# Feed-forward columns computed feature-major instead of token-major in a three-layer fp32 block kernel

## The reference

```
def _rmsnorm(x, w):
    x32 = x.astype(jnp.float32)
    y = x32 * lax.rsqrt(jnp.mean(x32 * x32, axis=-1, keepdims=True) + RMS_EPS)
    return (y * w.astype(jnp.float32)).astype(x.dtype)
...
u = _rmsnorm(h, norm_ffn_w[l])
hid = jax.nn.silu(jnp.einsum('btd,df->btf', u, w_ffn_gate[l])) * jnp.einsum('btd,df->btf', u, w_ffn_up[l])
h = h + jnp.einsum('btf,fd->btd', hid, w_ffn_down[l])
```

## Time and profile before

| | before |
|---|---|
| median of 3 runs | 2542.1 us |
| profiled execution | 2540.26 us, span 2538.5 us |
| TensorE products busy | 2493.6 us (98%), 14496 |
| TensorE weight loads busy | 2140.1 us (84%) |
| VectorE busy | 1802.3 us (71%) |
| ScalarE busy | 1154.8 us (45%) |
| mean granted clock of TensorE | 0.996 |
| DMA | 605.72 MB, 239 GB/s |

### The profile page before, as it was taken

One profiled execution on the slowest core, in us unless ns is written; L12 is line 12 of the kernel. 1 busy time (PEld: TensorE's weight loads), 2 busy tenths in 40 slices (PEclk: granted clock), 3 DMA queues, 4 the chain that ended last, 5 costly groups with the idle time before them and its releaser, 6 DMA issues.

```text
span 2538.5 us, 38110 instructions
## 1 busy us (share of the span) xinstructions
PE 2493.6 (98%) x14496; PEld 2140.1 (84%) x14496; DVE 1802.3 (71%) x2341; ACT 1154.8 (45%) x1476; POOL 0.2 (0%) x4
## 2 busy tenths in 40 slices
PE   8999999999999999999999999999999999999998
PEld 8977888788888888888888888899988788999886
DVE  6897676776677877777777777777786665546666
ACT  5544333464544544444443334433486344335642
POOL 0000000000000000000000000000000000000000
PEclk9999999999999999999999999999999999999999
DMA  7777676786778888888887788888745556675464
GB/s 218 247 248 255 213 256 217 264 272 215 254 237 268 286 286 283 284 282 282 282 286 259 261 262 263 279 288 282 248 141 185 183 175 185 188 235 181 133 219 146
DMA packets 317516, 605.72 MB, mean 239 GB/s; under 512 B 27310, under 2 KB 31412, under 8 KB 315708
## 3 DMA queue, kind: packets, MB, share of 16 engines
q1 hardware_dynamic: 301628, 571.59, 69.6%
q10 hardware_dynamic: 15744, 32.15, 3.6%
HBM read 593.03 MB, written 10.62 MB: 238 GB/s over the span
## 4 chain that ended last, share of the span: by engine, by line
PE 90%; DVE 4%; ACT 2%; DMA 2%; issue 1%; ACTq 0%; SPq 0%; DVEq 0%
PE bank L681 22%; PE bank L683 22%; PE bank L682 22%; PE bank L706 5%; PE bank L708 5%; PE bank L707 5%; PE bank L624 2%; PE bank L811 1%; DVE w_lo L1960 1%; ACT w_hi L1308 1%; DVE conv_out L2108 1%; DMA gemv_w<-in_w_mod 1%; DVE gemv_acc L1979 1%; DMA gates<-spill 1%; PE bank L1144 1%
## 5 line engine op out<-in xcount | busy, mean ns | idle before, releaser
L1960 DVE TENSOR_TENSOR w_lo<-raw,w_hi 128x1024 fp32r<-128x1024 f32 x820 | 1001.8, 1224 | 658.9 <-ACT w_hi L1308 656.8
L1308 ACT CAST w_hi<-raw 128x1024 fp32r<-128x1024 f32 x820 | 860.2, 1051 | 1290.2 <-PE bank L683 953.2
L681 PE MATMUL bank<-w_hi,u_hi 128*128 128x512 f32 x1216 | 483.5, 398 | 0.1
L683 PE MATMUL bank<-w_hi,u_lo 128*128 128x512 f32 x1216 | 474.3, 390 | 0.0
L682 PE MATMUL bank<-w_lo,u_hi 128*128 128x512 f32 x1216 | 474.0, 390 | 0.0
L1979 DVE SCALAR_TENSOR_TENSOR gemv_acc<-gemv_w,small,gemv_acc 128x512 f32<-128x512 f32 x480 | 358.8, 747 | 30.6 <-DMA gemv_w<-in_w_mod 25.3
L681 PE MATMUL bank<-w_hi,s_hi 128*128 128x512 f32 x744 | 297.9, 400 | 1.8 <-DVE w_lo L1960 1.7
L683 PE MATMUL bank<-w_hi,s_lo 128*128 128x512 f32 x744 | 291.4, 392 | 0.0
L682 PE MATMUL bank<-w_lo,s_hi 128*128 128x512 f32 x744 | 290.7, 391 | 0.0
L706 PE MATMUL bank<-s_hi,w_hi 128*128 128x256 f32 x1024 | 287.8, 281 | 0.3 <-DVE w_lo L1960 0.3
L707 PE MATMUL bank<-s_lo,w_hi 128*128 128x256 f32 x1024 | 287.6, 281 | 0.0
(11 more groups left out here) (365 smaller groups left out, 2858.9 us busy)
## 6 DMA issues: line engine op xcount, KB each, us to landing
gemv_w<-in_w_mod SPq DMA_DIRECT2D x384, 256.0 KB, 3.3
raw<-in_w_in SPq DMA_DIRECT2D x176, 512.0 KB, 4.5
raw<-in_a_w_in SPq DMA_DIRECT2D x128, 512.0 KB, 4.6
raw<-in_w_ffn_gate SPq DMA_DIRECT2D x88, 512.0 KB, 4.6
raw<-in_w_ffn_up SPq DMA_DIRECT2D x88, 512.0 KB, 4.6
raw<-in_w_ffn_down SPq DMA_DIRECT2D x88, 512.0 KB, 4.3
gemv_w<-in_kv_w_mod SPq DMA_DIRECT2D x128, 256.0 KB, 3.7
raw<-in_kv_w SPq DMA_DIRECT2D x64, 512.0 KB, 3.7
```

Of the source, the lines that this page charges most:

```text
L681: pe.matmul(o, xh, w_hi[pr.ring][:, s, t], start=(k == 0), stop=False)
L683: ins = pe.matmul(o, xl, w_hi[pr.ring][:, s, t], start=False, stop=(k == 2 * units - 1))
L1308: act.copy(w_hi[ahead.ring][:, s], raw[:, s]).then_inc(hi_done, 1)
L1960: dve.tensor_tensor(w_lo[ring][:, s], raw[:, s], w_hi[ring][:, s].bitcast(F32), ALU.subtract).then_inc(lo_done, 1)
```

## The change

The product "ffn" goes the second way. A body still computes one chunk of gate columns and one of up columns from the same weights, but now with 24 products of 256 columns in a unit in place of 12 of 512, and the four blocks of 128 hidden features come out with features on partitions, as down needs them. The transposes of `stage`, their PSUM banks and the waits for them are gone.

The root is now needed along the free dimension, on all partitions. VectorE writes a diagonal matrix for each half of the tokens (`root_diag`, identity times root), TensorE multiplies it with a matrix of ones behind unit 6 of the first body, and VectorE copies the result to `root_rows`. Both chunks are multiplied with it as they leave PSUM (`times_root`); ScalarE takes Silu of the gate chunk in place in slot 9, VectorE multiplies both at the end of the body, ScalarE casts the result in slot 2 of the next body and VectorE takes the low part in slot 4. `root_rows` lies where the causal mask and the not yet used `modc` lie, so the mask is loaded again before v2. Several semaphores are shared under new names (`staged`, `split_high`, `split_low`, `small_sum`).

```diff
+        root_rows = place("root_rows", [P, T], F32, at[0] + 4 * CAUSAL)
         keep = place("keep", [P, KEEP_W], F32)
+        modc = place("modc", [P, P], F32)
         cols = place("cols", [P, 3 * P], F32)
-        modc = place("modc", [P, P], F32)
...
+        root_diag = stage_all[:, 2 * COLS:2 * COLS + T]
+        hidden = stage[:, 1].rearrange("p h c -> p (h c)").rearrange("p (f t) -> p f t", t=T)
...
-            ("ffn", FF // COLS, 16, 2), ("down", 2, KF, 0),
+            ("ffn", FF // COLS, 16, 0), ("down", 2, KF, 0),
-        PASSES_ACROSS = ("qkv", "k2", "q2", "k3", "q3")
+        PASSES_ACROSS = ("qkv", "ffn", "k2", "q2", "k3", "q3")
...
                     if j == 1 and first:
                         last_x("w_out", "ffn")
-                    elif j == 3 and not first:
-                        turn_stage(pr, i - 1, 1)
-                chunk(pr, i, 0, u2_hi, u2_lo, pr.units // 2, due, {6: pr.turn0} if first else None)
-                chunk(pr, i, 1, u2_hi, u2_lo, pr.units // 2, due)
+                    elif j == 6 and first:
+                        pe.wait_ge(signal("over_root"), HALVES)
+                        pe.matmul(bank[SPARE][:, 0:T], ones, root_diag, start=True, stop=True).then_inc(signal("small_sum"), 1)
+                across_chunk(pr, i, 0, u2_hi, u2_lo, due, {6: pr.turn0} if first else None)
+                across_chunk(pr, i, 1, u2_hi, u2_lo, due)
...
                 if j == 3:
-                    turn_stage(pr, pr.bodies - 1, 1)
                     first_mods()
+                if j == KF // 2 - 3:
+                    pe.wait_ge(signal("split_low"), H1 + pr.bodies)
...
-            def silu_gate(pr, i, x):
-                if x == 0:
-                    act.wait_ge(signal("over_root"), 1)
-                    for th in range(HALVES):
-                        act.activation(stage[:, 0, th], acc[0][th][:], ACT.Silu, scale=sm(RR + th)).then_inc(drained[0], 1)
+            def silu_gate(j, i):
+                if j == 9:
+                    act.wait_ge(drained[0], i * 2 + 2 * (pr.body0 + 1))
+                    act.activation(stage[:, 0], stage[:, 0], ACT.Silu).then_inc(signal("gates_open"), 1)
             def hidden_high(j, i):
-                if j == 4:
-                    his_of_stage(products["ffn"], i, 1, hid_hi)
+                if j == 2:
+                    act.wait_ge(signal("staged"), i + (HALVES * products["branch"].bodies + 1))
+                    act.copy(hid_hi[:, ds(i * 4, 4)], hidden).then_inc(signal("split_high"), 1)
...
+            act.dma_start(keep[:, CAUSAL:CAUSAL + P], keep_const[:, CAUSAL:CAUSAL + P]).then_inc(signal("dist_in"), 16)
             act.dma_start(dist[:], keep_const[:, DIST:DIST + T]).then_inc(signal("dist_in"), 16)
...
                 if j == HALVES + 2:
                     dve.wait_ge(signal("root_x"), 2)
-                    dve.reciprocal(sm(RR, HALVES), sm(RR, HALVES)).then_inc(signal("over_root"), 1)
-            def times_gate(pr, i, x):
+                    own.link(dve.reciprocal(sm(RR, HALVES), sm(RR, HALVES)))
+                    for th in range(HALVES):
+                        dve.tensor_scalar(root_diag[:, th * P:(th + 1) * P], ident, sm(RR + th), None, ALU.mult).then_inc(
+                            signal("over_root"), 1)
+                if j == HALVES + 5:
+                    dve.wait_ge(signal("small_sum"), 2)
+                    own.link(dve.tensor_copy(root_rows[:], bank[SPARE][:, 0:T]))
+            def times_root(pr, i, x):
+                for half in range(2):
+                    dve.tensor_tensor(two_blocks(stage[:, x, half]), two_blocks(acc[x][half][:]), over_heads(root_rows[:], 2),
+                                      ALU.mult).then_inc(drained[x], 1)
                 if x == 1:
-                    dve.wait_ge(signal("over_root"), 1)
-                    dve.wait_ge(drained[0], i * 2 + 2 * (pr.body0 + 1))
-                    for th in range(HALVES):
-                        dve.scalar_tensor_tensor(out=stage[:, 1, th], in0=acc[1][th][:], scalar=sm(RR + th),
-                                                 in1=stage[:, 0, th], op0=ALU.mult, op1=ALU.mult).then_inc(drained[1], 1)
+                    dve.wait_ge(drained[1], i * 2 + 2 * (pr.body0 + 1))
+                    dve.wait_ge(signal("gates_open"), i + (2 * products["branch"].bodies + 1))
+                    dve.tensor_tensor(stage[:, 1], stage[:, 1], stage[:, 0], ALU.mult).then_inc(signal("staged"), 1)
             def hidden_low(j, i):
                 if j == 4:
-                    los_of_stage(products["ffn"], i, 1, hid_lo, hid_hi)
+                    blocks_of = ds(i * 4, 4)
+                    dve.wait_ge(signal("split_high"), i + (H1 + 1))
+                    dve.tensor_tensor(hid_lo[:, blocks_of], hidden, hid_hi[:, blocks_of].bitcast(F32), ALU.subtract).then_inc(
+                        signal("split_low"), 1)
...
-            dve.wait_ge(signal("dist_in"), 16)
+            dve.wait_ge(signal("dist_in"), 32)
```

More of the change, by code:

```diff
@@ L854, in delta_net @@
                 pe.matmul(bank[SPARE][0:H1, 0:T], small[0:BUCKETS, RELB:RELB + H1], early[0:BUCKETS, ONEHOT:ONEHOT + T],
-                          start=True, stop=True).then_inc(signal("rel_sum"), 1)
+                          start=True, stop=True).then_inc(signal("small_sum"), 1)
                 yield from rest(10)
@@ L1129, in down_first @@
                 if j == 3:
-                    turn_stage(pr, pr.bodies - 1, 1)
                     first_mods()
+                if j == KF // 2 - 3:
+                    pe.wait_ge(signal("split_low"), H1 + pr.bodies)
                 if j == products["down"].units // 2 - 1:
                     mod_columns(0)
-            turning_x("down", hid_hi, hid_lo, "v2", down_first, {KF // 2 - 2: pr.turn0 + pr.bodies * pr.turns})
+            pe.wait_ge(signal("split_low"), H1 + pr.bodies - 1)
+            turning_x("down", hid_hi, hid_lo, "v2", down_first, None)
             def scores2(p, a):
@@ L1585, in yb_high @@
                 act.wait_ge(signal("b_out"), h + 1)
-                act.copy(yb_hi[:, h], bank[OUTS][:, 0:T]).then_inc(signal("yb_high"), 1)
+                act.copy(yb_hi[:, h], bank[OUTS][:, 0:T]).then_inc(signal("split_high"), 1)
             def rows_in(hg):
@@ L1723, in norm_due, with first_ffn, ffn_due @@
                     root(0, sm(SS, HALVES), sm(RR, HALVES), 1.0 / D, E6, "root_x")
[L1725 to L1736 removed]
+            def silu_gate(j, i):
+                if j == 9:
+                    act.wait_ge(drained[0], i * 2 + 2 * (pr.body0 + 1))
+                    act.activation(stage[:, 0], stage[:, 0], ACT.Silu).then_inc(signal("gates_open"), 1)
+            def hidden_high(j, i):
+                if j == 2:
+                    act.wait_ge(signal("staged"), i + (HALVES * products["branch"].bodies + 1))
+                    act.copy(hid_hi[:, ds(i * 4, 4)], hidden).then_inc(signal("split_high"), 1)
+            def first_ffn(j):
+                norm_due(j)
+                silu_gate(j, 0)
+            def ffn_due(j, i):
+                hidden_high(j, i - 1)
+                silu_gate(j, i)
+            body("ffn", 0, nothing, first_ffn)
             with act.Fori(1, pr.bodies - 1) as i:
[L1738 removed]
+                body("ffn", i, nothing, lambda j: ffn_due(j, i))
             last = pr.bodies - 1
[L1740 removed]
+            body("ffn", last, nothing, lambda j: ffn_due(j, last))
             def mod_rows_in(n):
@@ L2480, in hidden_low @@
             def hidden_low(j, i):
                 if j == 4:
-                    los_of_stage(products["ffn"], i, 1, hid_lo, hid_hi)
-            body("ffn", 0, times_gate, norm_due)
+                    blocks_of = ds(i * 4, 4)
+                    dve.wait_ge(signal("split_high"), i + (H1 + 1))
+                    dve.tensor_tensor(hid_lo[:, blocks_of], hidden, hid_hi[:, blocks_of].bitcast(F32), ALU.subtract).then_inc(
+                        signal("split_low"), 1)
+            body("ffn", 0, times_root, norm_due)
@@ L2485, in _ @@
             with dve.Fori(1, pr.bodies - 1) as i:
-                body("ffn", i, times_gate, lambda j: hidden_low(j, i - 1))
+                body("ffn", i, times_root, lambda j: hidden_low(j, i - 1))
             last = pr.bodies - 1
-            body("ffn", last, times_gate, lambda j: hidden_low(j, last - 1))
+            body("ffn", last, times_root, lambda j: hidden_low(j, last - 1))
             def mod_columns(n):
```

24 lines of the change are left out of this document (11 added, 13 removed).

## The result

The changed kernel took 2551.1 us (median of 8 runs, 2547.8 to 2554.2), the kernel before, in turn with it, 2540.0 (8 runs, 2535.6 to 2543.9): a ratio of 1.0045, 95% interval 1.0034 to 1.0055. It is slower by 0.45%, where 2532.5 and "faster" stood in the forecast as the likeliest. The slow-pace rival had 2550.9.

A forecast was written before the change was run, and what follows sets the result against it. The prediction took TensorE's pace to bound the kernel. Its terms, -9.1 - 0.9 + 1.8 + 0.3 + 0.1, summed to -7.8 us, from the profiled execution's 2540.3 us to 2532.5; the whole range was 2527 to 2553.

The forecast's parts named there:

- slow-pace rival: The feed-forward loop keeps 0.1178 us a product, +0.82 us a body, +10.6 in all, 2550.9 us; chance 0.27.
- the fast one: The feed-forward loop runs at 0.1133 us a 256-column product, giving 2532.5 us; chance 0.58.
- three of three unbroken entries: Evidence for the slow pace: slow stretches in the earlier trace were entered from other products without a pause.
- 1. Loop bodies: Ten feed-forward loop bodies take 43.5 us against 44.42, the transposes gone: -9.1 us.
- 2. The last turn in down: The same eight transposes go at unit 3 of down: -0.9 us.
- 3. First body: In the first feed-forward body casts wait one unit longer for the other ring, delaying the turn of x: +1.8 us.
- 4. Root's product: One plain fp32 product of 256 columns at unit 6 of the first body: +0.3 us, bounds 0.1 and 0.6.
- 5. VectorE: VectorE's work per loop body goes from 33.9 to 36.2 us of 43.5; cost 0 with 2.9 us to spare.
- 6. ScalarE: In the loop, one Silu and one 1024-column cast replace two of each; with 24 us idle, cost 0.
- 7. v2: One more 64 KB DMA ahead of dist, which VectorE waits for: between 0 and +0.5 us, taken as 0.1.
- Instruction fetch: The loop body's 786 TensorE instructions are not held, so nine jumps each wait for a block: +18 us, 2550; chance 0.10.
- The edge: VectorE or a transfer comes late at the loop body's end; 1 us a body gives 2542.5 us; chance 0.05.

The follow-up runs named there:

- one_each: The changed kernel with one unread identity transpose behind unit 3 of each feed-forward loop body; 2551.2 us.
- one_all: As one_each, with one such transpose also behind unit 3 of each body of k2, q2, k3 and q3; 2543.0 us.
- root_plain: The changed kernel with the root's product made as two one-pass products of the same kind as the products around it; 2551.4 us.
- plain_one: root_plain plus single transposes behind unit 3 of each body of k2, q2, k3 and q3; 2533.5 us.
- no_root_product: The changed kernel without the product that spreads the root, the row of roots filled with ones; 2533.5 us.
- turns_each: The changed kernel with eight identity transposes behind unit 3 of every feed-forward loop body; 2545.3 us.
- turns_ahead: The changed kernel with eight unread identity transposes between the first feed-forward body and the loop; 2538.5 us.
- turns_once: The changed kernel with eight identity transposes behind unit 3 of the second feed-forward body alone; 2539.6 us.
- once_one: turns_once plus single transposes behind unit 3 of each body of k2, q2, k3 and q3; 2528.1 us.

## Why the prediction was wrong

**The step that failed** is the choice of the pace. The prediction named both paces, priced both, and wrote that "it decides at the root's product"; then it took the fast one, since "a transpose is of the same plain kind". The root's product is not of the same kind for this: it is drawn as two instructions (x2), a transpose as one. The trace before held the sign: the line of the earlier trace rows has 16 such products and the row counts 32. In the seven traces with the four-byte product at these addresses, the stretch behind the turn of x is fast in five and slow in two, and the stretch behind the root's product is slow in all seven. Without that product the loop ran fast in the profile and in eight of ten runs by their times. Of the kernels that have the product and no eight transposes behind it (changed kernel, one_each, one_all), none of 24 runs lies in a fast group; with the product made of its neighbours' kind 12 of 24 do (root_plain, plain_one).

The sentence that "behind transposes the pace is fast" was a second fault: it rested on one turn. The window read there, 22 to 25 us, even counts transposes of the next turn among its 27.6 products; by their starts (113.3 ns apart) the pace was fast all the same. But behind the very same turn in the code it is fast in six of the fourteen traces and slow in eight. Eight transposes make a toss here. Even with the root's product out of the way the forecast would have held in some of the runs only; root_plain has 5 of 12, and its median of 2551.4 is as slow as the changed kernel's. What had weighed against the fast pace, three of three unbroken entries, was the better evidence.

Term by term:
1. Loop bodies: -9.1 in the fast pace; measured 10 x (45.23 - 44.42) = +8.1. In no_root_product it is 10 x (43.52 - 44.42) = -9.0. Both prices in the prediction were right, and the wrong one was taken.
2. The last turn in down: -0.9, measured -0.9.
3. First body: +1.8. The turn begins 826.73 - 818.99 = 7.74 us into the stage, before it was 821.57 - 815.62 = 5.95: +1.8, as worked out, and with the fast pace (no_root_product) the whole first body is 482.3 - 435.2 = 47.1 us for 489.5 - 444.2 = 45.3, again +1.8. What was missed is the clock. The stand of 1.93 us is followed by 3.4 us on the lower level, and from the turn's start to the tenth product behind it it takes 3.59 us, where turns_each, with the same stand, the slow pace and the full clock, takes 1.99: +1.6, and unit 6 started 21.6 us into the stage for the 19.9 of the forecast (19.8 in no_root_product). The fall of the clock does not happen in every run: of the ten traces with a stand of 1.92 or 1.93 us seven have the lower level behind it and three, no_root_product's among them, have not. With the lower clock, the slow pace of the other units and the root's product the first body is 4.9 us longer.
4. Root's product: +0.3 with bounds of 0.1 and 0.6; the second product behind it starts 0.55 us after its own start, where without it that would be 0.12: +0.43. The size was right; that it would leave something behind was not in it.
5. VectorE: 36.2 us a body; measured 35.7, with 682, 1225 and 1219 ns for the three new kinds against 680 and 1224. No wait for low parts in the loop.
6. ScalarE 18.9 us a body, cost 0.
7. v2: 88.1 and 88.1, cost 0.

**The slow-pace rival** summed to +10.6; measured +11.2 between the medians, +10.2 between the spans. That it is so near holds some luck: the half clock (+1.6) and the start of the kernel (+3.4) are not in it, and the -5.2 of k3 and q3 in this execution is the other way. **Instruction fetch**: bodies of 786 TensorE instructions jump without a gap, and q8 brings 2 blocks in 422 us. The rival is out. The Trainium skill (Runtime: NRT & Kernel Launch, Instruction fetch mechanics) has the rule by which only two blocks are held and a jump out of them stalls; for TensorE this trace disagrees with it, and the measurement decides. **The edge**: no wait of TensorE in any loop body. The shares given (0.58, 0.27, 0.10, 0.05) had fast and slow the wrong way round.

**What stays open.** Why the plain fp32 product leaves TensorE slow is not shown. In the traces the distance from the first to the second product behind an interruption goes along with the pace in part: 305 ns behind the root's product and slow; behind transposes at the full clock 200 and 201 are slow in 20 of 24 cases, 202 and 203 are fast in 38 of 57, 204 to 206 are fast in all 13. This is no rule. Nor is it shown what decides the toss from run to run, or why it falls fast ten times of ten in turns_each. Runs without a profile are put in a group by their time alone.

## What to carry to other kernels

When the same instruction has two paces in one trace at the same clock, the pace is a state with an entry, and a change that removes "useless" instructions may remove what let the engine leave the slow one: list what stands before every stretch of each pace, and give the unbroken, counted entries more weight than a likeness of kind. If one product of another kind goes into a long gapless stream, this case puts the bet on the slow side. A few transposes that nobody reads can pay for themselves many times over (0.1 us each for 6 us in k2 and q2), but in the loop and in k3 and q3 they only toss or worse, so compare whole distributions of runs, since a single profile shows one side.

## What the runs showed of the hardware

- A 256-column product with its own weight load has three paces at the full clock: 113.3 ns (drawn 276), 117.8 (drawn 281), and 120.0 (drawn 283) with the weights 64 bytes lower. The first two are held over up to 4075 products. The Trainium skill (TensorE: Matmul & The Clock Gate, Back-to-back issue gap) gives 262 cycles at this width for an isolated product; at 2.4 GHz that is 109 ns, an estimate from the page's figure. No stretch here reached it.
- A kernel's runs then fall into two groups, their middles 16 to 24 us apart (turns_ahead, root_plain, plain_one, turns_once, once_one: 7 us or more without a run between them), at the same granted clock.
- Behind a stand of 1.9 us the clock was at its lower level for 3.4 us in seven traces and stayed full in three, in kernels that differ nowhere up to there.
